# Block-Toeplitz taps of the S5 mixer stored already shifted, from ScalarE's DMA queue, and read back in one transfer a tile; first S5 tables loaded during the last slots of the second down projection

## The reference

```python
u = (h @ w_in).astype(f32)
...
def step(carry, u_c):
    bu_re = jnp.einsum('gpc,bkgc->bkgp', bb_re, u_c)
    bu_im = jnp.einsum('gpc,bkgc->bkgp', bb_im, u_c)
    ...
    _, _, x_re, x_im = lax.associative_scan(
        _complex_linear_combine, (a_seq_re, a_seq_im, bu_re, bu_im), axis=1)
    y = (jnp.einsum('gcp,bkgp->bkgc', c_re, x_re)
         - jnp.einsum('gcp,bkgp->bkgc', c_im, x_im))
    return (x_re[:, -1], x_im[:, -1]), y
...
y = y + d_skip.astype(f32) * u
y = jax.nn.gelu(y).astype(h.dtype)
y = y * jax.nn.sigmoid(y @ w_glu)
return y @ w_out
```

## Time and profile before

| | |
|---|---|
| median of 3 runs | 1803.36 us (1802.19 to 1805.9) |
| the profiled execution | 1800.33 us, its span 1798.6 us |
| mean granted TensorE clock | 0.969 of 2.4 GHz |
| DVE, ACT, POOL busy | 57%, 36%, 13% of the span |
| DMA | 212.7 MB, 118 GB/s over the span |
| first down projection with tables | about 382 to 526 us of the span |
| second one | about 1093 to 1228 us |
| S5 stage up to the gate's last parts | about 1228 to 1363 us |

### The profile page before, as it was taken

How to read it: one execution, slowest core, us unless ns; L and a number is a source line. 1 busy time by engine, 2 the same in 40 slices (tenths; PEclk the granted TensorE clock), 3 DMA queues, 4 the chain that set the end, 5 groups by cost and what they waited for, 6 DMA issues and landing times.

```text
span 1798.6 us, 22087 instructions
## 1 busy us (share of the span) xinstructions
PE 1692.3 (94%) x8681; PEld 1410.4 (78%) x8681; DVE 1031.1 (57%) x1551; ACT 639.8 (36%) x992; POOL 237.0 (13%) x757
## 2 busy tenths in 40 slices
PE   3649999999999999999999999999989999999998
PEld 2638888888877787878888888888868888888886
DVE  5887866676665677676433335757736633333223
ACT  3334533332243565554322222334214522222222
POOL 5001240000006754650000000000010000000000
PEclk7579999999999999999999999999989999999999
DMA  9352323234433122213322334467763233223332
GB/s 379 134 229 83 100 92 102 94 106 143 127 103 116 62 67 67 65 42 97 115 96 94 95 99 129 113 181 223 235 180 117 82 108 104 94 94 95 104 95 70
DMA packets 138151, 212.69 MB, mean 118 GB/s; under 512 B 29904, under 2 KB 104000, under 8 KB 134848
## 3 DMA queue, kind: packets, MB, share of 16 engines
q1 hardware_dynamic: 123392, 204.98, 35.8%
q10 hardware_dynamic: 14656, 6.29, 1.2%
HBM read 193.43 MB, written 17.82 MB: 117 GB/s over the span
## 4 chain that ended last, share of the span: by engine, by line
PE 86%; DVE 6%; DMA 3%; POOL 1%; ACT 1%; SPq 1%; issue 1%; ACTq 0%; DVEq 0%; PEldq 0%; POOLq 0%
PE bank L1748 26%; PE bank L1750 26%; PE bank L1749 26%; DVE ada L1177 2%; DMA rcnt<-in_rcnt 1%; PE bank L1788 1%; PE bank L2013 1%; PE bank L1879 1%; PE bank L2044 1%; PE bank L2150 1%; PE bank L1986 1%; DMA u_scratch<-us 1%; DVE w_lo L1091 1%; SPq L663 1%; DMA raw<-in_fox_in 1%
## 5 line engine op out<-in xcount | busy, mean ns | idle before, releaser
L1748 PE MATMUL bank<-hh,w_hi 128*128 128x512 f32 (+1 forms) x1440 | 558.1, 388 | 7.7 <-DVE w_lo L1091 2.9
L1749 PE MATMUL bank<-hl,w_hi 128*128 128x512 f32 (+1 forms) x1440 | 548.8, 381 | 0.0
L1750 PE MATMUL bank<-hh,w_lo 128*128 128x512 f32 (+1 forms) x1440 | 548.5, 381 | 0.0
L1091 DVE TENSOR_TENSOR w_lo<-raw,w_hi 128x1024 fp32r<-128x1024 f32 x264 | 318.2, 1225 | 197.2 <-ACT w_hi L740 194.5
L740 ACT ACTIVATE w_hi<-raw 128x1024 fp32r<-128x1024 f32 x264 | 277.6, 1056 | 380.5 <-PE bank L1750 123.3
L1748 PEld LDWEIGHTS bank<-hh,w_hi 128*128 128x128 f32 x1440 | 272.4, 189 | 64.4 <-issue 7.9
L1749 PEld LDWEIGHTS bank<-hl,w_hi 128*128 128x128 f32 x1440 | 272.5, 189 | 54.3 <-issue 3.8
L1750 PEld LDWEIGHTS bank<-hh,w_lo 128*128 128x128 f32 x1440 | 272.3, 189 | 51.7
L1748 PE MATMUL bank<-w_hi,hid 128*128 128x512 f32 x528 | 206.9, 392 | 0.0
L1750 PE MATMUL bank<-w_hi,hid 128*128 128x512 f32 x528 | 205.6, 389 | 0.0
L1749 PE MATMUL bank<-w_lo,hid 128*128 128x512 f32 x528 | 205.4, 389 | 0.0
(11 more groups left out here) (271 smaller groups left out, 2039.5 us busy)
## 6 DMA issues: line engine op xcount, KB each, us to landing
raw<-in_up SPq DMA_DIRECT2D x132, 512.0 KB, 3.3
raw<-in_dn SPq DMA_DIRECT2D x60, 512.0 KB, 4.0
ada<-in_ada_w SPq DMA_DIRECT2D x24, 1024.0 KB, 9.9
raw<-in_fox_in SPq DMA_DIRECT2D x32, 512.0 KB, 3.5
raw<-in_s_w SPq DMA_DIRECT2D x24, 512.0 KB, 4.5
q_scratch<-q_tab SPq DMA_DIRECT2D x8, 512.0 KB, 4.3
w_scratch<-w_new SPq DMA_DIRECT2D x8, 512.0 KB, 5.1
raw<-in_fox_out SPq DMA_DIRECT2D x8, 512.0 KB, 3.8
```

What stands on the lines that cost most here:

```text
L1091: dve.tensor_tensor(w_lo[:, n % RING, :], raw[:, n % RING, :], w_hi[:, n % RING, :].bitcast(F32), ALU.subtract).then_inc(lo_done, 1)
L1748: pe.matmul(dst, w_h, r_h, start=first, stop=False, skip_group_check=True)
L1749: pe.matmul(dst, w_h, r_l, start=False, stop=False, skip_group_check=True)
L1750: return pe.matmul(dst, w_l, r_h, start=False, stop=last, skip_group_check=True)
```

## The change

The taps are stored shifted. After `skip_taps` ACT (no longer SP) issues eight stores for each tile, at slot index 4t+6, behind `hi` of that index and ahead of everything else of it. They fill the whole 128-partition Toeplitz tile in DRAM, 512 KB instead of 120 KB. `w3_load` becomes one DMA of 512 KB. SP's order is rewritten: the first loads of `w1`, `turn`, `w3` (tiles 0 to 3) and `q2` (tiles 0 to 2) are issued with the last four down slots, as soon as their part of `hid` has been used, and the later ones at other places of S5.

```diff
-        k_dram = nc.dram_tensor("k_scratch", (KT, CH, 8, KW), F32, kind="Internal").ap()
+        k_dram = nc.dram_tensor("k_scratch", (KT, P, 8, P), F32, kind="Internal").ap()
...
                         sp.dma_start(w1_dram[i], w1_new[:, :, :, :].rearrange("p a b c -> p (a b c)")).then_inc(w1_out, 16)
-                        sp.wait_ge(kd_done, i + 1)
-                        sp.dma_start(k_dram[i], kt[0:CH, :, :]).then_inc(k_out, 16)
...
+            def w3_load(i):
+                if i >= TABS:
+                    sp.wait_ge(w3_mm, i - TABS + 1)
+                sp.dma_start(w3[:, i % TABS, :, :].rearrange("p g j -> p (g j)"),
+                             k_dram[i].rearrange("p g j -> p (g j)")).then_inc(w3_in[i % TABS], 16)
...
+                    if t0 and idx >= HALF_DN + 8:
+                        early_tables(idx - HALF_DN - 5)
+
+            def early_tables(idx):
+                sp.wait_ge(slot_mm, S_DN2 + HALF_DN + idx + 1)
+                if idx == 3:
...
+                    for i in range(2):
+                        w1_load(i)
+                        turn_load(i)
+                    sp.wait_ge(k_out, 16 * BLK * KT // 2)
+                    w3_load(0)
+                if idx == 4:
+                    w3_load(1)
+                    w3_load(2)
+                if idx == 5:
+                    w3_load(3)
+                    sp.wait_ge(q_out, 16 * KT // 2)
+                    q2_load(0)
+                if idx == 6:
+                    q2_load(1)
+                    q2_load(2)
...
-            sp.wait_ge(slot_mm, S_S5I - TAIL)
-            sp.wait_ge(turn_out, 16 * PAIRS // 2)
-            for i in range(2):
-                w1_load(i)
-                turn_load(i)
-            for i in range(2):
-                w3_load(i)
-                q2_load(i)
+            early_tables(HALF_DN - TAIL - 1)
             for idx in range(1, RING):
                 load_fm(S_S5I + idx, dram["s5_w"][idx])
-            w3_load(2)
-            sp.wait_ge(k_out, 16 * KT)
+            q2_load(3)
+            sp.wait_ge(k_out, 16 * BLK * KT)
...
-                if i == 0:
-                    w3_load(3)
-                if i == 1:
-                    q2_load(2)
-                if i == 3:
-                    q2_load(3)
+                if i == 4:
+                    w3_load(4)
+                    w3_load(5)
                 if i == 5:
-                    w3_load(4)
+                    q2_load(4)
                     y_write(sp, 0)
-                    w3_load(5)
                     y_read(sp, 0)
                 if i == 6:
-                    q2_load(4)
+                    w3_load(6)
+                    w3_load(7)
             y_write(sp, 2)
             q2_load(5)
             y_read(sp, 2)
-            w3_load(6)
-            w3_load(7)
...
+            def tap_store(i):
+                act.wait_ge(kd_done, i + 1)
+                rows_of = k_dram[i].rearrange("(c s) g j -> s c g j", s=BLK)
+                for s in range(BLK):
+                    at_s = KPAD - CH * s
+                    act.dma_start(rows_of[s], kt[0:CH, :, at_s:at_s + P]).then_inc(k_out, 16)
+
             def down(q, first, t0=None):
                 for idx in range(DNS):
                     hi(first + idx + LEAD)
+                    if t0 is not None and idx - 6 in TABLE_SLOT:
+                        tap_store(t0 + (idx - 6) // 4)
                     if idx == DNS - TAIL:
                         break
```

More of the change, by code:

```diff
@@ L601, in load_s5_matrices, with w1_load, turn_load, q2_load @@
                 sp.dma_start(cc[:, :, :, :], dram["s5_c"]).then_inc(s5_big, 16)
+            def w1_load(i):
+                if i >= 2:
+                    sp.wait_ge(st_mm, i - 1)
+                sp.dma_start(w1[:, i % 2, :, :, :].rearrange("p a b c -> p (a b c)"), w1_dram[i])\
+                  .then_inc(w1_in[i % 2], 16)
+            def turn_load(i):
+                if i >= 2:
+                    sp.wait_ge(rec_done, i - 1)
+                sp.dma_start(turn[:, i % 2, :, :].rearrange("p t c -> p (t c)"),
+                             turn_dram[i].rearrange("p t r j -> p (t r j)")).then_inc(turn_in[i % 2], 16)
+            def w3_load(i):
[3 more added lines that the diff above has]
+                             k_dram[i].rearrange("p g j -> p (g j)")).then_inc(w3_in[i % TABS], 16)
+            def q2_load(i):
+                if i >= TABS:
+                    sp.wait_ge(out_mm, i - TABS + 1)
+                sp.dma_start(q2[:, i % TABS, :, :, :].rearrange("p a b c -> p (a b) c"), q_dram[i])\
+                  .then_inc(q2_in[i % TABS], 16)
             def down_loads(first, dn, t0=None):
@@ L609, in down_loads @@
                         tables_at(idx, first, t0)
+                    if t0 and idx >= HALF_DN + 8:
[3 more added lines that the diff above has]
+                if idx == 3:
+                    sp.wait_ge(w1_out, 16 * KT // 2)
+                    sp.wait_ge(turn_out, 16 * PAIRS // 2)
+                    for i in range(2):
[13 more added lines that the diff above has]
+                    q2_load(2)
             down_loads(S_DN1, dram["dn1"], 0)
@@ L787, in boundary @@
                             act.wait_ge(q_out, 16 * 4 * (q // 2 + 1))
-                            act.wait_ge(k_out, 16 * 4 * (q // 2 + 1))
+                            act.wait_ge(k_out, 16 * BLK * 4 * (q // 2 + 1))
                         evict_h(q, b - 1)
@@ L839, in store_tables @@
                     act.wait_ge(w1_out, 16 * i)
-                    act.wait_ge(k_out, 16 * i)
+                    act.wait_ge(k_out, 16 * BLK * i)
                 for t in range(2):
@@ L2145, in inside @@
                 p = i % TABS
-                pe.wait_ge(w3_in[p], 16 * BLK * (i // TABS + 1))
+                pe.wait_ge(w3_in[p], 16 * (i // TABS + 1))
                 if i >= 4:
```

21 lines of the change are left out of this document (removed).

## The result

The changed kernel takes **1820.3 us** (median of 6 runs, 1817.95 to 1821.34) against 1802.78 us (median of 6, 1800.37 to 1805.9) for the kernel before on the same chip: ratio 1.0102, 95% interval 1.009 to 1.0114, some 18 us slower. I go by the ratio. All ratios are of fast executions; one of kernel 12, 5990 us long, is left out of its row. The forecast was 1807.8 us with 1792 to 1815 as its range. The sign was right, the size was not.

The account below looks back on a forecast made before the run. PE bounds the kernel, busy 94% of the span, so edits act through its stands and low clock. Loss 19.4 minus S5 gain 15.0 is +4.4 us, added to 1803.36 for 1807.8 us; range 1792 to 1815 for 8 in 10.

Parts of the forecast that it names:

- the four places: Index 10 and index 18 (boundary) of both down projections: PE stands 4.0, 4.25, 2.5 and 3.4 us.
- Part 3: Down projections: eight tap stores hold ACT 4.8 us and stall PE, 14.15 us idle plus 5.25 us clock; loss 19.4 us.
- Rival (a): Down projections: eight stores hold ACT only 2.5 us, stalls sum to 4.95 us, no clock fall; 1793 us, chance 0.22.
- Rival (c): Down projections: stores land late, delaying next `store_tables` and index 10 stalls; net +10.6, 1814 us, chance 0.10.
- Part 2: First tables loaded over the last down slots, ahead of later slots' weights: costed at nothing, up to 2 us.
- Part 1: S5: eight `w3` loads become one and SP's order changes, so waits and low clock go; gain 15.0 us (13 to 17).
- All are more than 3 us before their need: S5 loads for tiles 6 and 7 leave SP early enough that `w1` and `w3` waits of 2.9 + 6.3 us go.
- the terms for the clock: S5: time at 1.2 GHz after the waits comes back, 1.8 and 3.75 us in two windows.
- POOL's split: First `glu_part` of S5: PE arrives before POOL's split ends, a new wait of 0 to 2.5 us, taken as 1.2.
- Rival (b): S5 gate inputs: held `yfm` copies make PE wait, `ub` not won; gain 10.5, net +9, 1812 us, chance 0.10.
- rival (d): S5 `w3` waits had another releaser, so the loss stands without most of the gain; 1818 us, chance 0.03.
- The prediction's own signs: Changed profile: S5 clock not 1.00 refutes Part 1; `hl` over 2 us means Rival (b); later t=1 `store_tables`, Rival (c).

Follow-up runs that it names:

- kernel 12: kernel 7 with the loads of `w1` for tiles 6 and 7 and `q2` of tile 4 cut to 16 partitions; 1795.98 us, ratio 0.9977.
- kernel 3: The changed kernel with the same eight stores a tile issued by POOL instead of ACT; 1800.17 us, ratio 1.0002.
- Kernel 6: kernel 3 with the first tables loaded after the down slots, where they were before, keeping the new S5 order; 1798.3 us, ratio 0.9980.
- kernel 11: kernel 4 with the loads of `w1` for tiles 6 and 7 and `q2` of tile 4 cut to 16 partitions; 1793.46 us, ratio 0.9965.
- kernel 4: Kernel before with part 1 alone: shifted storage by POOL, one `w3` load a tile, old SP order, no early tables; 1795.65 us, ratio 0.9969.
- kernel 7: kernel 4 with ACT's two `yfm` copies moved ahead of the read of u tile 7; 1796.34 us, ratio 0.9972.
- kernel 13: kernel 7 with ACT's eviction and write of u tile 6 moved ahead of its reads of `yfm`; 1795.53 us, ratio 0.9970.
- kernel 10: kernel 4 with SP waiting until u tile 6 has landed before weights ahead of `w1` of tile 7; 1797.95 us, ratio 0.9985.

## Why the prediction was wrong

**Bound and places: right.** All losses are stands of PE or its low clock, and the four places were those named.

**Part 3, loss 19.4 us: right in mechanism, and in size by one of two measures.** By the ratios of the change and of kernel 3 it is 18 us. By the trace of the change alone it is the 24.6 us of the down projections, 5 more than forecast. The two differ because kernel 3 stands 2.45 us for weights behind the early tables, with low clock behind it, while the changed kernel's PE, held by ACT, comes later and stands 0.43 us at that place.

The eight issues took 4.53 to 5.28 us where I had 4.8; the stands were 5.92, 5.28, 2.47 and 4.11 us, 17.8 in all, where I had 4.0, 4.25, 2.5 and 3.4, 14.15. The squares and the last multiply took 3.4 us, not 2.95. What the two down projections lost beyond their stands (11.2 + 13.4 - 17.8) is 6.8 us, where I had 5.25 for the clock.

Rival (a), the cheap issue, is refuted. The page of the Trainium skill that the prediction set beside it, "DMA: Bandwidth & Descriptors", says in "Issuing engines are not separate DMA queues" that spreading DMAs over engines saves only the issue time, which is usually small relative to the DMA itself. Taken one by one the trace agrees, 0.54 us an issue on ACT against 4.7 us to its landing; but small beside the DMA is not small in its place, and moving the same issues from ACT to POOL was worth 18 us. The table with the 50 ns stands in the same page of the Trainium skill under "Anatomy of one DMA — SWDGE (gpsimd) path", so for DMAs that POOL issues, and the prediction applied it to ACT; POOL's issues in kernel 3 took 0.53 us each.

**Rival (c) happened too,** in part: the stores landed after 4.7 us in the median, not 2.9, ACT waited for them four times, 10.6 us in all, and the stand of 5.92 us holds 1.8 from it. In the second down projection it did nothing at index 10, but before the last tile ACT waited 5.44 us, and against PE's arrival at the boundary the last `skip_taps` is 1.2 us later than before, which is part of the stand of 4.11 us.

**Part 2, nothing (up to 2 us): wrong.** By kernels 3 and 6 it costs about 4 us. The step that failed is "needed some 10 us later": the loads of down slots 20 and 21 had this slack only while nothing stood before them. The five loads of 2 MB took it, less by their issuing than by the landing behind them, 9.3 and 10.7 us in kernel 3 against 7.3 and 6.4 before.

**Part 1 and the new order, gain 15.0 us: wrong, and this is most of the error.** Kernel 6, which has both and neither of the other parts, gains 0.2% (0.1 to 0.3%), 3.6 us. The step that failed is "All are more than 3 us before their need, so 2.9 + 6.3 us go" for the `w1` wait, and with it the terms for the clock (5.55 us) and for `ub` (1.5 us). The `w3` waits, 6.3 us, did go.

The instruction that waited for `w1` waits for `ub` of the same tile as well. Before, that landed at 1291.83 + 3.5 = 1295.3, and I took it as settled. But it landed early while SP was held by the very loads that the change removes; with SP free it took 7.7 us, and in kernel 11, with SP free and three of its loads small, 3.8. I had asked what is late next, and looked only at POOL's split (1.2 us; it was 2.27). Nor did the clock come back: both profiles have two stretches of S5 at 1.2 GHz, some 3.6 and 10.4 us long by the sum on the windows.

In waits: 1.53 + 2.89 + 3.37 + 2.93 + 1.60 = 12.3 us before, 0.20 + 1.57 + 2.71 + 2.27 + 1.61 = 8.4 after, 3.9 less. Rival (b) named the right place and the `ub` wait, and priced the gain that is left at 10.5 us; it was 5.0. The time nearest to the measured one, 1818, stood at rival (d), but by chance: it wanted the `w3` waits to stay, and they are gone. The prediction's own signs had it right: the clock in S5 did not go to 1.00, `hl` was waited for over 2 us, and `store_tables` of t=1 started later.

**The sum** by ratios: 18 + 4 + 2 (order) - 5.6 (part 1 alone) = 18.4 us, of 1802.8. This adds up by construction, since each term is the difference of two kernels, and the terms depend on the order in which the parts are added; the term of the order of S5 is within its uncertainty. By the traces the error is 5 us in the down projections and 10 in S5.

**What stays open.** With the waits in the middle of S5 taken away one after the other, the single profiles of kernels 4, 7, 11, 12 and 13 show the stage shorter by 6 to 10 us, while their medians lie at 1793.5 to 1796.3 us. Runs of one of these kernels differ by 3 to 9 us, and the granted clock fell in each profile, at different places. In kernel 10's one profile the stage is as long as before, 197.7 us, with the `ub` wait there gone and the clock low for some 20 us. That the clock takes back what a removed wait gives is what this execution looks like; it isn't shown for the medians. So which waits stood in S5 is shown, and why taking them away pays so little is not.

## What to carry to other kernels

Cost a DMA by the line it stands in: multiply its issue time (here about 0.5 us on ACT, SP and POOL alike) by the count, ask what stands behind it on that engine and how long before its need that work was done, and give it to an engine with nothing behind it. When an edit frees a queue, list the transfers that will now start earlier and the small round trips they will run beside; a landing time read from the old trace holds only for the old traffic. Where an instruction waits for several things, look up when each of the others came before you book the gain.

## What I had not expected of the hardware

- The time to issue doesn't grow with the bytes: 0.56 us for 904 KB, 0.54 us for 64 KB (medians on ACT). The landing does: 11.3 and 4.7 us, though eight of 64 KB in a row took 6.8 to 12.0 us from the first issue to the last landing.
- A 256 KB round trip through DRAM is elastic: over all the traces the write of a u tile landed in 2.2 to 8.3 us and the read in 2.7 to 11.5 us. Taking 1.3 MB of the bulk loads beside it away brought one read from 10.4 to 3.8 us.
- The granted clock can be at 1.2 GHz for most of 20 us in which PE is busy for 19.69, and in the changed kernel it fell at 1303 with no stand over 0.31 us in the 15 us before. A stand of 2.47 us in the first down projection was followed by no fall. An idle time and the clock loss after it were not in a fixed proportion.
